# A transformer kernel whose first mixer scales its heads in another order and turns its rows in two halves, and whose last layer computes a gate behind a copy

## The reference

```
# first block, layer 0 (mixer one)
proj = rms_norm(x, g) @ w_in                      # q, k, v of 6 heads, q of 4 memory heads
s = q_m @ k_m.T * scale + bias                    # two score maps m = 0, 1 a head
a = softmax(s_0) - lam * softmax(s_1)
o = a @ v                                         # (256, 6, 128)
o = rms_norm(o, subln_g) * (1.0 - lam_init)       # a row's mean square, then a gain
om = softmax(qm @ km.T * scale) @ vm              # memory attention, 256 wide
x = x + concatenate([o, om], -1) @ w_out
x = x + dense_swiglu(rms_norm(x))
# layer 1: recurrent mixer, then 8 experts, top 2
# second block
proj = modulate(rmsnorm(x), ...) @ w_in           # gq, gk, gv, gr, gg, mq, mk, mv
log_a = log_sigmoid(gg @ w_gla_gate + b) / 16     # the gate
o_gla = gla_mixer(gq, gk, gv, log_a) ; o_moba = moba_mixer(mq, mk, mv)
x = x + gate_a * (concatenate([o_gla, o_moba]) @ w_out) ; x = x + gate_m * mlp(x) ; rmsnorm(x)
```

## Time and profile before

| | |
|---|---|
| median of 3 runs | 1820.73 us (1819.74 to 1821.03) |
| profiled execution, its own time | 1820.13 us |
| its span in the profile | 1818.3 us |
| PE busy | 1764.0 us, 97% |
| DVE / ACT busy | 1410.4 us, 78% / 1115.3 us, 61% |
| POOL busy | 127.8 us, 7% |
| mean granted clock | 0.987 |

### The profile page before, as it was taken

One profiled execution on the slowest core, in us unless ns is written; L12 is line 12 of the kernel. 1 busy time (PEld: TensorE's weight loads), 2 busy tenths in 40 slices (PEclk: granted clock), 3 DMA queues, 4 the chain that ended last, 5 costly groups with the idle time before them and its releaser, 6 DMA issues.

```text
span 1818.3 us, 22247 instructions
## 1 busy us (share of the span) xinstructions
PE 1764.0 (97%) x8369; PEld 1444.6 (79%) x8369; DVE 1410.4 (78%) x1226; ACT 1115.3 (61%) x1025; POOL 127.8 (7%) x156
## 2 busy tenths in 40 slices
PE   8979999999999999999999999999999989999998
PEld 6867888788768888888888888888888857778886
DVE  5556778857769888888888888888888976475556
ACT  5654444453557777777777777777777755543333
POOL 3011111112130000000000000000001010000000
PEclk9989999999999999999999999999999999999999
DMA  9636899754169999999999999999999974535550
GB/s 319 204 127 214 278 338 317 263 165 139 61 223 376 383 383 383 376 388 380 379 384 376 380 387 375 388 369 378 375 376 392 393 272 162 151 120 205 185 185 24
DMA packets 237420, 525.96 MB, mean 289 GB/s; under 512 B 17066, under 2 KB 40810, under 8 KB 237184
## 3 DMA queue, kind: packets, MB, share of 16 engines
q1 hardware_dynamic: 223376, 477.23, 72.8%
q0 software_dynamic: 13936, 47.32, 7.7%
HBM read 513.95 MB, written 10.53 MB: 288 GB/s over the span
## 4 chain that ended last, share of the span: by engine, by line
PE 90%; DVE 4%; ACT 2%; DMA 2%; issue 1%; SPq 0%; DVEq 0%; ACTq 0%
PE bank L2787 27%; PE bank L2788 27%; PE bank L2795 27%; DVE w_lo L1673 1%; PE bank L3227 1%; ACT w_hi L1054 1%; PE bank L2937 1%; PE bank L2850 1%; DMA raw<-in_moe_w_down 1%; PE bank L2899 1%; DMA raw<-in_moe_w_gate_up 1%; PE bank L2843 1%; DMA raw<-in_a_w_mem_kv 1%; PE bank L3585 0%; PE bank L2868 0%
## 5 line engine op out<-in xcount | busy, mean ns | idle before, releaser
L1673 DVE TENSOR_TENSOR w_lo<-raw,w_hi 128x2048 fp32r<-128x2048 f32 x453 | 1040.8, 2300 | 222.5 <-ACT w_hi L1054 209.1
L1054 ACT ACTIVATE w_hi<-raw 128x2048 fp32r<-128x2048 f32 x453 | 867.3, 1916 | 473.9 <-PE bank L2788 336.6
L2787 PE MATMUL bank<-w_hi,slot_hi 128*128 128x512 f32 x896 | 355.2, 396 | 0.9 <-DVE slot_lo L2322 0.9
L2788 PE MATMUL bank<-w_hi,slot_lo 128*128 128x512 f32 x896 | 349.3, 390 | 0.0
L2787 PE MATMUL bank<-w_hi,hT_hi 128*128 128x512 f32 (+1 forms) x704 | 279.5, 398 | 6.9 <-DVE hT_lo L1738 2.5
L2788 PE MATMUL bank<-w_hi,hT_lo 128*128 128x512 f32 (+1 forms) x704 | 274.7, 391 | 0.0
L2795 PE MATMUL bank<-w_lo,slot_hi 128*128 128x512 f32 x896 | 240.6, 390 | 1.6 <-DVE w_lo L1673 1.6
L2795 PEld LDWEIGHTS bank<-w_lo,slot_hi 128*128 128x128 f32 x896 | 167.7, 188 | 38.9 <-DVE w_lo L1673 4.0
L2787 PEld LDWEIGHTS bank<-w_hi,slot_hi 128*128 128x128 f32 x896 | 168.3, 188 | 34.5 <-DVE slot_lo L2322 1.1
L2788 PEld LDWEIGHTS bank<-w_hi,slot_lo 128*128 128x128 f32 x896 | 168.5, 188 | 33.2
L2795 PE MATMUL bank<-w_lo,hT_hi 128*128 128x512 f32 (+1 forms) x704 | 174.9, 391 | 0.0
(11 more groups left out here) (426 smaller groups left out, 1445.2 us busy)
## 6 DMA issues: line engine op xcount, KB each, us to landing
raw<-in_moe_w_gate_up SPq DMA_DIRECT2D x448, 512.0 KB, 5.6
raw<-in_moe_w_down SPq DMA_DIRECT2D x224, 512.0 KB, 5.7
raw<-in_w_ff SPq DMA_DIRECT2D x64, 512.0 KB, 4.4
work<-in_w_ada POOLq DMA_DIRECT2D x48, 512.0 KB, 5.4
raw<-in_dense_w_gate_up SPq DMA_DIRECT2D x44, 512.0 KB, 5.1
raw<-in_b_w_in SPq DMA_DIRECT2D x24, 512.0 KB, 5.4
raw<-in_w_in SPq DMA_DIRECT2D x24, 512.0 KB, 5.3
raw<-in_dense_w_down SPq DMA_DIRECT2D x22, 512.0 KB, 4.7
```

Source lines behind the costliest of these rows:

```text
L1054: act.activation(w_hi[:, g % SPLIT, 0:n], raw[:, g % RING, 0:n], ACT.Copy).then_inc(R.hi, 1)
L1673: dve.tensor_tensor(w_lo[:, g % SPLIT, 0:n], raw[:, g % RING, 0:n], f32(w_hi[:, g % SPLIT, 0:n]), ALU.subtract).then_inc(R.lo, 1)
L2787: pe.matmul(out_, hi, w_hi[:, s, c:c + w], start=(start and n == 0), stop=False, skip_group_check=True)
L2788: mm = pe.matmul(out_, lo, w_hi[:, s, c:c + w], start=False, stop=False, skip_group_check=True)
```

## The change

In mixer one POOL multiplies each head's columns of `mix` by the gain, as soon as `value_out` has written them (six operations, 128x2x128). DVE then scales two heads at a time by the reciprocal alone (three operations of 128x2x256 in place of twelve of 128x128), so that the roundings come in another order. On ACT only one unit of `a_out` is made early, behind item 3's copy; the other is made behind the first two groups of `hT_hi`. The exponentials of the last item stand ahead of the table load, and the load ahead of item 6's copies. The last item's transposes go to banks 6 and 3 and stand ahead of item 6's value products. PE turns groups 0 and 1 of `mix` ahead of the last item's value products, and groups 2 and 3 inside the first unit of `a_out`, between its two output banks. `turn_probs` gets a parameter `idle` for filler matmuls, which no call uses. In the last layer `gate()` stands behind `split_hi(in2(1, 1))` and `leave_in(0)`.

```diff
@@ mixer one's items
+        a_items[-1].turns_in = [bank[6], bank[3]]
@@ gpsimd, behind the nine transfers of y_zero
+            if have("diff"):
+                pool.wait_ge(gain_in[0], 16)
+                for i in range(DA_HEADS):
+                    pool.wait_ge(*at(f"diff{i}", "out"))
+                    o = mix[:, :, i * P:(i + 1) * P]
+                    pool.tensor_tensor(o, o, gain[:, 0, 0:P].unsqueeze(1).broadcast_to([P, TILES, P]), ALU.mult)\
+                        .then_inc(S("diff", "weighted", i), 1)
@@ scalar
                 exponentials(a_items[1], None)
-                begin("a_out")
                 for n in range(1, DA_HEADS):
                     exponentials(a_items[n + 1], at(f"diff{DA_HEADS - 2}", "turned") if n + 1 == DA_HEADS else None)
                     turned_out(a_items[n], at(f"diff{n - 2}", "values") if n >= 2 else None)
+                    if n == 3:
+                        split_hi(ring, G["a_out"], 0)
+                exponentials(a_items[DA_HEADS + 1], None)
+                load_sqrt()
                 turned_out(a_items[DA_HEADS], at(f"diff{DA_HEADS - 1}", "scores"))
-                exponentials(a_items[DA_HEADS + 1], None)
                 head_norm("diff")
                 turned_out(a_items[DA_HEADS + 1], None)
...
-                turn_split("mix_a", G["a_out"])
+                act.wait_ge(ring.used, G["a_out"])
+                for n in range(2):
+                    mix_hi(n)
+                split_hi(ring, G["a_out"] + 1, 0)
+                for n in range(2, 4):
+                    mix_hi(n)
                 product("a_out", None)
@@ scalar, in_2
-                gate()
                 split_hi(ring, in2(1, 1), 0)
                 leave_in(0)
+                gate()
                 split_hi(ring, in2(2, 0), 0)
@@ vector
-                head_scale("diff", 0, lambda h, t: 2 * h + t)
-                for it in a_items[DA_HEADS:]:
-                    value_out(it)
+                for h in range(0, DA_HEADS, 2):
+                    for i in range(h, h + 2):
+                        dve.wait_ge(*at("diff", "weighted", i))
+                    o = mix[:, :, h * P:(h + 2) * P].rearrange("p t (h d) -> p t h d", d=P)
+                    r = headsq[:, 2 * h:2 * h + 4].rearrange("p (h t) -> p t h", t=TILES)
+                    dve.tensor_tensor(o, o, r.unsqueeze(3).broadcast_to([P, TILES, 2, P]), ALU.mult).then_inc(S("diff", "normed", h // 2), 1)
...
+                value_out(a_items[DA_HEADS])
+                for n in range(2):
+                    mix_lo(n)
+                value_out(a_items[DA_HEADS + 1])
+                S.also("mix_a")
             if have("a_out"):
-                turn_split("mix_a")
+                split_lo(ring, G["a_out"], 0)
+                for n in range(2, 4):
+                    mix_lo(n)
+                split_lo(ring, G["a_out"] + 1, 0)
...
-                product("a_out", True, behind=early_dense)
+                product("a_out", True, behind=early_dense, ahead=1)
@@ tensor
-            def turn_probs(it, free):
+            def turn_probs(it, free, idle=0):
-                pe.wait_ge(*at(it.tag, "exp" if it.kind == "mem" else "mixed"))
                 if free is not None:
                     pe.wait_ge(*free)
+                if idle:
+                    run_idle(idle, 4 + it.n % 2)
+                pe.wait_ge(*at(it.tag, "exp" if it.kind == "mem" else "mixed"))
...
-                value_products(a_items[N - 1], None)
+                turn_probs(a_items[N - 1], at(f"diff{DA_HEADS - 2}", "out"))
+                value_products(a_items[N - 2], None)
...
-                turn_split("mix_a", mix, at("diff", "normed", 0),
-                           later={1: at("diff", "normed", 1), 2: at("diff", "normed", 2), 3: at("mix_a")})
+                def turn_mix(n):
+                    pe.wait_ge(*at(a_items[N - 1].tag, "copied"))
+                    pe.wait_ge(*(at("diff", "normed", n) if n < 3 else at("mix_a")))
+                    if n >= 2:
+                        pe.wait_ge(*at("mix_a", "taken", n - 2))
+                    turn_pair("mix_a", mix, n, 6 + n % 2)
+
+                def turn_second_half():
+                    for n in range(2, 4):
+                        turn_mix(n)
+
+                for n in range(2):
+                    turn_mix(n)
+                value_products(a_items[N - 1], None)
+                pe.wait_ge(*at(a_items[N - 2].tag, "out"))
...
-                product("a_out", "mix_a", after=early_x("a_out", "dense"))
+                product("a_out", "mix_a", None, turn_second_half, after=early_x("a_out", "dense"))
```

More of the change, by code:

```diff
@@ L1276, in _, with mix_hi @@
                 S.stage("a_out")
-                turn_split("mix_a", G["a_out"])
+                def mix_hi(n):
+                    act.wait_ge(*at("mix_a", "turned", n))
+                    act.activation(flat(hT_hi[:, 2 * n:2 * n + 2, :]), bank[6 + n % 2][:, :], ACT.Copy).then_inc(S("mix_a", "hi", n), 1)
+                act.wait_ge(ring.used, G["a_out"])
[4 more added lines that the diff above has]
+                    mix_hi(n)
                 product("a_out", None)
@@ L2043, in _, with mix_lo @@
                 dve.wait_ge(*S.last())
-                head_scale("diff", 0, lambda h, t: 2 * h + t)
-                for it in a_items[DA_HEADS:]:
-                    value_out(it)
+                for h in range(0, DA_HEADS, 2):
[4 more added lines that the diff above has]
+                    dve.tensor_tensor(o, o, r.unsqueeze(3).broadcast_to([P, TILES, 2, P]), ALU.mult).then_inc(S("diff", "normed", h // 2), 1)
+                S.also("gain used", 0)
+                def mix_lo(n):
+                    dve.wait_ge(*at("mix_a", "hi", n))
+                    dve.tensor_tensor(flat(hT_lo[:, 2 * n:2 * n + 2, :]), bank[6 + n % 2][:, :],
+                                      f32(flat(hT_hi[:, 2 * n:2 * n + 2, :])), ALU.subtract).then_inc(S("mix_a", "taken", n), 1)
+                value_out(a_items[DA_HEADS])
[3 more added lines that the diff above has]
+                S.also("mix_a")
             if have("a_out"):
-                S.also("mix_a")
                 S.stage("a_out")
-                turn_split("mix_a")
+                split_lo(ring, G["a_out"], 0)
+                for n in range(2, 4):
+                    mix_lo(n)
+                split_lo(ring, G["a_out"] + 1, 0)
                 def early_dense(j):
@@ L3066, in _ @@
                 scores(a_items[2], at(a_items[0].tag, "max"))
-                for n in range(1, N):
-                    if n + 2 < N:
-                        scores(a_items[n + 2], at(a_items[n].tag, "max"))
+                for n in range(1, N - 1):
+                    scores(a_items[n + 2], at(a_items[n].tag, "max")) if n + 2 < N else None
                     turn_probs(a_items[n], at(a_items[n - 1].tag, "copied") if n >= DA_HEADS else
```

## The result

| kernel | median us | executions | ratio to before, 95% interval |
|---|---|---|---|
| before | 1820.56 (1819.74 to 1821.03) | 4 | |
| changed | 1808.22 (1807.73 to 1808.77) | 4 | 0.9933 [0.9916, 0.9950] |

The profiled execution took 1807.73 us, 12.4 less than the one of before. First the page's part 1, which answers to the earlier trace rows.

A forecast was written before the change was run, and what follows sets the result against it. PE, busy 97% of the span, was taken as the bound, so time could come only from its idle and half-clock stretches. Gate 5.1 plus mixer one 1.0 made 6.1 us, giving 1814.6 us, range 1809.5 to 1818.5.

The forecast's parts named there:

- Term B: Last layer's gate: PE's idle 3.58 us and 1.49 us of half-speed matmuls behind it go, 5.1 us gained.
- rival of a delay one unit later: Last layer: block 1 copied 2 us or more late, gate gain 3 or below, time 1817; chance 0.07.
- Term A: Mixer one: four edits and the clock's part together gain 1.0 us, bounds -1.2 to +2.8.
- the clock does not fall: Mixer one: shorter PE idle time keeps the clock up, 6.6 us more gained, time 1808.7; chance 0.10.
- If the rise does not move: Mixer one: clock's rise at 143.8 stays, nothing added, or moves with the products, 1.1 us saved; 0.7 taken.
- ACT's two units: Mixer one: moving them from between two exponentials ends DVE's idle time ahead of a reciprocal, 0.85 us gained.
- POOL's products: Mixer one: gain products on POOL make DVE wait, 0.45 us for each of four heads, 1.8 us lost.
- rival of 1.0 each: Mixer one: each POOL collision with DVE costs 1.0 us, time 1817.5; chance 0.10.
- Order on ACT: Mixer one: earlier exponentials paid away by the table load ahead of item 6's copies; value products at 130.4 against 129.94, -0.45.
- Order on PE: Mixer one: PE's pause of 0.71 us among the transposes is filled by the last value products, +0.71.
- The cheaper scaling: Mixer one: DVE's twelve scaling operations lay under value products of 6.69 us, so cheaper scaling gives nothing.
- The turned rows delay the clock: Mixer one: transposes between two banks' matmuls keep the clock down longer, 1.6 us lost, time 1816.9; chance 0.13.

The follow-up runs named there:

- e1: Kernel before with only the gate moved behind the copy of block 0, mixer one untouched; median 1815.8 us, ratio 0.9970.
- e5: The changed kernel word for word, run again in more executions with another profile; median 1811.2 us, ratio 0.9937 against before.
- e2: Changed kernel with the gate back at its old place, all edits of mixer one kept; median 1817.5 us, ratio 0.9974 against before.
- f1: The changed kernel again, on one chip with the kernels compared to it; median 1811.1 us, ratio 0.9934 against before.
- e4: Kernel before with eight filler matmuls in PE's wait of 2.33 us ahead of the last item's transposes; median 1813.8 us, ratio 0.9957.
- e11: Kernel before with only ACT's two units for the mixer's product made later, as in the changed kernel; median 1817.9 us, ratio 0.9984.
- e6: Changed kernel with filler matmuls in PE's pauses of mixer one; median 1805.4 us, ratio 0.9909 against before.
- e7: Changed kernel with PE's pauses in mixer one filled and the old scaling back, no gain products on POOL; median 1806.4 us, ratio 0.9917 against before.
- f2: Changed kernel with the old scaling back and no gain products on POOL, beside the changed kernel on one chip; median 1807.4 us, ratio 0.9913 against before.
- e8: Changed kernel with ACT copying item 6's turned rows ahead of the last item's exponentials, table load behind those; median 1811.5 us, ratio 0.9941 against before.
- e10: Kernel before with eight filler matmuls in PE's wait of 2.33 us and the gate moved; median 1810.0 us, ratio 0.9945.
- e3: Changed kernel with the old scaling by DVE in twelve operations, no gain products on POOL; median 1807.1 us, ratio 0.9926 against before.
- e9: Changed kernel with groups 2 and 3 turned ahead of the first product, not between its two banks; median 1811.1 us, ratio 0.9947 against before.
- f4: Changed kernel with mixer one's pauses filled, again, on one chip with the changed kernel; median 1806.4 us, ratio 0.9906 against before.
- e12: Changed kernel with mixer one's pauses filled and eight more fillers in the first dense round; median 1807.3 us, ratio 0.9919 against before.

## Why the prediction was wrong

**Term B (gate, 5.1) was right.** In the profiles G fell from 22.92 to 17.52, 5.4 us: the two terms named (3.58 of idle time, 1.4 as the eight matmuls went from 3.47 to 2.09), and some 0.4 in the matmuls around them, of which those right behind ran at half clock too. Over other profiles with the gate at its old place G is 22.2 to 24.2, as the fall behind the pause is short or long; e1 gives 5.5 (0.9). The slack at block 1, forecast 0.6 us, was 0.7. The rival of a delay one unit later fell.

**Term A (mixer one, 1.0) was the step that failed**, by the clock's part in it. Take e5, whose execution lost 4.1 us in S where before lost 4.2, and in which the clock fell behind the copies as before. There the prediction's own steps come out roughly. Value products 0.15 us later than before (27.60 against 27.45; forecast 0.46). First wide product at 138.14 (138.4). Clock back at 140.7 (141.7 to 143.8; the part I had left at 0.7). `w_lo` matmuls at 143.98, 1.9 us ahead of before's 145.86. For such an execution A is 1.9, and 1.0 was only mis-sized. But where the clock stays up, P is 9.34 in place of 15.92, 6.6 us less, and this happened in two of three profiles of the changed kernel. Over all executions the mixer's edits are worth 4.8 (e2) to some 6 us (11.3 and 12.1 for e5 and f1, less 5.5 for the gate), in place of 1.0.

The rival "the clock does not fall", with a chance of 0.10, named the mechanism. That its price, 6.6, and its time, 1808.7, also fit is partly luck. It halved all 13.2 us of work, but at full clock PE waits more for DVE (1.35 us ahead of the second transposes in e4, 0.71 in before): the clock alone gave 5.2 us in P in the old order (15.92 to 10.75, e4) and 4.6 in the new (e5 against f1). The order and the scaling made up the rest (1.4, steps 4 and 5 below).

The step that failed stands in the sentence "If the rise does not move, nothing is added; if it moves with the products", and in the 0.7 us taken from it: it took the clock's course in one profiled execution as a property of the program, which an edit shifts or doesn't. Executions of one program differ in it: before lost 4.2 and e1 7.0 in S with the same instructions there, e5 lost 5.1 in P and f1 nothing, and before's times spread over 14 us.

By step:

1. *ACT's two units, 0.85.* Right only where the clock is down in that item. Where it is up, they cost 1.8 to 1.9 (DVE's wait in e4; PE's item in e4 against e11), and e11 measures 3.2 (0.9) with what the clock adds. The mistake was to price a delay by the last wait of a row, when another wait of 1.04, on PE at half clock, stood ahead of it and hid the rest.
2. *POOL's products, 4 x 0.45 = 1.8.* Nearly right: 1.54 in S with the pauses filled (e6 against e7), 1.3 to 1.8 at equal loss (e5 and f1 against f2), 0.36 to 0.43 for each of the four stretched operations, 1.5 in all. The rival of 1.0 each fell. The Trainium skill, "SBUF — State Buffer", section "Who interferes with whom", describes the exclusive lock by which whoever comes second waits; the DVE operation at 107.66, which ends with POOL's product (107.58 + 0.72 = 108.30), agrees.
3. *Order on ACT.* The -0.45 is the net of the first three steps: the first two alone make the value products 0.95 later, and the order brings them 0.5 forward again. Not contradicted: by it S would be 27.45 + 0.46 = 27.91 at equal loss, and it is 27.60 in e5 and 28.10 in f1. e8 shows no difference in the mean.
4. *Order on PE, 0.71.* About right at full clock. P goes from 10.75 (e4, e10) to 9.34, 1.4 us for this step and the next together. With the old scaling the new order takes 10.20 to 10.23 (f2, e3), so the order itself, ACT's with it, gives 0.5. The halves are worth 0.56 of the 1.4 (e9).
5. *The cheaper scaling "gives nothing"*: wrong by 0.9 us (9.34 against 10.20 to 10.23), since its cover of 3 us was half-speed value products. At full clock and in the changed order PE waits for DVE there.
6. *The turned rows delay the clock.* It fell: in e5 the clock rose ahead of those transposes, within the first eight wide matmuls, and in the changed kernel's first profile it stayed at 1.00 through the transposes from 129.88 and from 134.68. By the Trainium skill, "TensorE: Matmul & The Clock Gate", Part 4, transposes don't engage the full clock as matmuls do. No row here shows them raising it; the rows show only that they let it stand. The other half of the prediction's reading, that the level doesn't rise in 64-column products, is not general: in e11 the granted clock is 0.50 from 126 to 128 and 1.00 from 129 on, in the middle of the 32 value products (126.43 to 131.0).

What isn't settled: how much of the mean gain each edit has through the clock. e11, e3 and e4 each raise the mean clock (0.989, 0.994 and 0.993 against 0.986). A profile's stretches don't give their mean gains: S and P together are 4.7 us shorter in e4, which gained 7.9, and 6.5 shorter in e11, which gained 3.2. Which pause brings the clock down in which execution no run tells.

## What to carry to other kernels

Before a clock-bound edit is priced, look at more than one execution. Add up busy time times one minus granted clock over the windows, list where it is lost, and treat entries ahead of and behind the change as the spread of the measurement; price an edit for the execution with the clock up and the one with it down, and weigh the two. Price a delay by the work that causes it, not by the last wait that is left of it. And a pause of a busy PE that can't be removed can be filled with matmuls whose result nobody reads: eight of them gave 7.9 us here, more than the edits of mixer one. Not every pause pays: filling one more, of 2.42 us in the dense layer (e12), gave nothing that could be measured.

## What the runs showed of the hardware that was not expected

The granted clock's falls aren't fixed by the program alone. The same pause brought the clock down in one execution and not in another (1.33 us ahead of the value products: up in the changed kernel's first profile and in f1, down in e5 and e2; 2.49 us in e12 and f4, above). In 28 executions of the kernel before the time followed the mean clock by 1.17 us for each 0.001, from 1812.1 us at 0.994 to 1826.5 at 0.983. With filler matmuls in every larger pause of S it was 1.00 throughout S and P in all four such profiles (e6, f4, e7, e12).
